# The first layer's input read by columns from memory, and its first query and key blocks walked together

## The chip, the core and the metric

The kernel runs on one core of a Trainium2 chip. TensorE (PE) multiplies, ScalarE (ACT) rounds and evicts, VectorE (DVE) makes remainders, masks and small transposes, GpSimd (POOL) rotates queries and keys and makes some remainders, and SyncE (SP) issues nearly all transfers. The metric is the time of one execution in device microseconds. Before the change the median of three runs is 840.39 us (839.6 to 840.73).

## The reference, cut to what matters

```
hn   = rms_norm(x, pre_norm_g[0])                  # x: 256 rows x 2048 columns, float32
proj = hn @ attn_w_in                              # 2048 x 8192
q, k, v, z = split(proj, 4)                        # 16 heads of 128 columns each
q, k = rope(q), rope(k)
o = causal_softmax(q k^T / sqrt(128)) v
x = x + rms_norm((o * silu(z)) @ attn_w_out, post_norm_g[0])
# then a second layer: gated convolution over 31 rows, layer norm, silu gate, w_out, again added to x
```

The root mean square scales a row, so it can be applied after the product: the kernel multiplies x times the gain by the weights, and scales each row when the sums leave PSUM. What the change touches is the head of this: how x comes in, how it is turned, and when the row scale is known.

## The kernel before, in words

All products are float32 in three passes: each operand is split into a rounded part (hi, written by ACT) and the remainder (lo, written by DVE, or by POOL in some later stages), and PE adds hi*hi, hi*lo and lo*hi. The weights stream through `raw` (four buffers of 1 MB, one SP transfer each), and are split by *slices*: a slice is two tiles of 128 rows of the inner dimension by 512 columns, so a buffer holds two slices. Eight slices make one block of 512 columns; a slice is 12 products of 512 columns. Each slice has one of four slots in `w_hi` and `w_lo`, so ACT can start on slice s only when PE has finished slice s-4. A slice's number below counts from 0 within a group.

The first layer goes through four groups of four heads. In a group, slices 0 to 7 make the queries, 8 to 15 the keys, 16 to 23 the values, 24 to 31 the gate. The order of each engine's work is written out by hand, slice by slice. In a group, ACT scales and evicts the query block (`block_rows`, lines 809 to 815) once it is complete; POOL then turns it by the rope tables (`rotate`, lines 1577 to 1597: four products with the sines, two with the cosines, one sum); DVE transposes the result in four steps of four 32-row transposes, one step behind each of four slices' remainders, beginning at slice `TURN_Q`. The keys follow in the same way with `TURN_K`. DVE runs in order: when a step waits for POOL, the remainder of the next slice waits behind it, and PE waits for that remainder.

In the first group the start is special. x comes in rows, PE turns it (`input_T`, four transposes of 128 by 128 for each pair of tiles), ACT writes `xT_hi` from PSUM with the gain, DVE `xT_lo`. The first two slices are done tile by tile (`FINE = 2`, `tile_products`), the next two by passes (`staged_products`). ACT squares the rows of x in between (eight pieces, two for each quarter of the columns) for the row scale; DVE sums them (`mean_of_parts`), POOL takes the inverse root into `rms[0]`, and the query block is evicted only then. Gains, biases and convolution taps come in by rows and are turned by PE as well.

Of the kernel before, what the change touches and what calls it, by code (L numbers as in the profile page):

```python
# [23 lines left out]
P = 128  # L24
SEQ = 256
D = 2048
# [27 lines left out]
NVEC = 5 * KT  # L54
ROOT_AT = 27
# [5 lines left out]
SPLIT_AFTER = ((), (), (2,), (3,), (4, 5), (6,), (7, 8), (9,))  # L61
FINE = 2
SQUARES_AFTER = (1, 2, 3, 5)
STAGED = 4
# [21 lines left out]
DW_ROWS = TAPS * KT // 4  # L86


def build(nc, x, pre_g, post_g, w_in0, w_out0, w_in1, b_in, w_dw, b_dw, ln_g, ln_b, w_out1, b_out,
# [5 lines left out]
    with ctx:  # L95
# [27 lines left out]
        uT_lo = at("uT_lo", B + 16 * KB, [P, KT, SEQ], f32r)  # L123
        c_row = at("c_row", B, [P, MT, D])
# [30 lines left out]
        vec_rows = at("vec_rows", C, [NVEC, P])  # L155
        dw_rows = at("dw_rows", C + 512, [DW_ROWS, 4, P])
        pre_rows = at("pre_rows", C + 2 * KB + 512, [NPRE, P])
# [38 lines left out]
        tile_in = [sem(f"tile_in{i}") for i in range(2 * FINE - 1)]  # L196
        half_in = sem("half_in")
        x_in = [sem(f"x_in{i}") for i in range(6)]
        tile_xhi, tile_xlo = sem("tile_xhi"), sem("tile_xlo")
        tile_whi, tile_wlo = sem("tile_whi"), sem("tile_wlo")  # L200
        tile_T = sem("tile_T")
        ident_in = sem("ident_in")
        pre_in = sem("pre_in")
        vec_in = sem("vec_in")
        dw_in = sem("dw_in")
# [3 lines left out]
        vec_T = sem("vec_T")  # L209
        vec_ready = sem("vec_ready")  # L210
# [93 lines left out]
        def x_chunk(h):  # L304
            return h if h < 4 else 2 + h // 2

        def of_tile(t, even, pair, count):

            return (even, t // 2 + 1) if t % 2 == 0 else (pair, count)

# [9 lines left out]
        def _(sp):  # L320
# [15 lines left out]
            def x_load(first, last):  # L336
                c = slice(first * SEQ, (last + 1) * SEQ)
                sp.dma_start(xrow[:, :, c], xv[:, :, c]).then_inc(x_in[x_chunk(first)], 16)

            def w_load(n, first, last, done):  # L340

                k = 2 * SL_K * n
                sp.dma_start(raw[:, n, first:last + 1], wv[:, k + first:k + last + 1, 0:NCOL]).then_inc(done, 16)
# [6 lines left out]
            w_load(0, 2, 2, tile_in[2])  # L350
            w_load(0, 3, 3, raw_ready[0])
            x_load(2, 2)
            w_load(1, 0, 1, half_in)
            x_load(3, 3)
            w_load(1, 2, 3, raw_ready[1])
            x_load(4, 5)
            load(S_QKVZ, 0, 32, 2, w_in0[0], 0)
            x_load(6, 7)
            load(S_QKVZ, 0, 32, 3, w_in0[0], 0)
            load(S_QKVZ, 0, 32, 4, w_in0[0], D)  # L360

            for v, rows, src in ((V_BA, 2 * KT, b_in), (V_BDW, KT, b_dw), (V_LNG, KT, ln_g), (V_LNB, KT, ln_b)):
                sp.dma_start(vec_rows[v - NPRE:v - NPRE + rows, :], src.rearrange("l (t c) -> (l t) c", c=P)
                             ).then_inc(vec_in, 16)
# [3 lines left out]
            sp.dma_start(dw_rows[:], w_dw[0].rearrange("k (t c) -> (k t) c", c=P)  # L368
                         .rearrange("(q r) c -> r q c", r=DW_ROWS)).then_inc(dw_in, 16)

            for j in range(5, 16):
                load(S_QKVZ, 0, 32, j, w_in0[0], (j // 4) * D)
# [63 lines left out]
        def _(pe):  # L436
# [54 lines left out]
            def input_T(layer, h):  # L491

                if layer == 0:
                    pe.wait_ge(x_in[x_chunk(h)], 16)
                    if h == 1:
                        pe.wait_ge(vec_ready, 1)
                    if h >= 4:
                        pe.wait_ge(xlo_ready, h - 3)
                else:
                    for m in range(MT):  # L500
                        pe.wait_ge(x1_ready[m], h + 1)
                    pe.wait_ge(xlo_ready, units(h - 4, 1))
                if layer == 0 and h < FINE:
                    for t in (2 * h, 2 * h + 1):
                        for m in range(MT):
                            last = nc.tensor.transpose(X[t][:, m * P:(m + 1) * P], xrow[:, m, t * P:(t + 1) * P],
                                                       ident[:])
                        last.then_inc(xT_done if t % 2 else tile_T, 1)
                else:
                    pair_T(xrow, X[h % 4], 2 * h).then_inc(xT_done, 1)  # L510

            def staged_products(h):

                slot = h % RING
                n = h + 1
                passes = [(xT_hi, w_hi, ((xhi_ready, n), (hi_ready[slot], rounds(S_QKVZ, 0, 0, h)))),
                          (xT_lo, w_hi, ((xlo_ready, n),)),
                          (xT_hi, w_lo, ((lo_ready[slot], rounds(S_QKVZ, 0, 0, h)),))]
                for p, (xs, ws, needs) in enumerate(passes):
                    for which, count in needs:  # L520
                        pe.wait_ge(which, count)
                    for i in range(SL_K):
                        k = SL_K * h + i
                        for m in range(MT):
                            last = nc.tensor.matmul(acc[:, 0, m], xs[:, k, m * P:(m + 1) * P],  # L525
                                                    ws[:, slot, i], start=(k == 0 and p == 0), stop=False)
                last.then_inc(w_used[slot], 1)

            def tile_products(t):
# [3 lines left out]
                passes = [(xT_hi, w_hi, (of_tile(t, tile_xhi, xhi_ready, n), of_tile(t, tile_whi, hi_ready[slot], 1))),  # L533
# [11 lines left out]
            def first_block():  # L545

                tile_products(0)
                input_T(0, 1)
                tile_products(1)
                tile_products(2)  # L550
                input_T(0, 2)
                tile_products(3)
                input_T(0, 3)
                for h in range(FINE, SLICES):
                    if h < STAGED:
                        staged_products(h)
                    else:
                        pe.wait_ge(xlo_ready, h + 1)
                        slice_products(S_QKVZ, 0, 32, h, xT_hi, xT_lo)
                    if h + 2 < SLICES:  # L560
                        input_T(0, h + 2)
# [38 lines left out]
            def group(g, first):  # L600

                for s in range(SLICES if first else 0, 4 * SLICES):
                    if s % SLICES == 0 and not (first and s < 2 * SLICES):
                        pe.wait_ge(rows_out, 4 * g + s // SLICES - 1)
                    slice_products(S_QKVZ, g, 32, s, xT_hi, xT_lo)
                    if s == VALUES_AT and not first:
                        values(g - 1)
                    if s == 9 and first:
# [1056 lines left out]
```

## Time and profile before

| | |
|---|---|
| median of three runs | 840.39 us |
| the profiled execution | 840.96 us |
| its span, first to last instruction | 839.2 us |
| PE busy | 829.8 us, 99% of the span |
| DVE busy | 713.0 us, 85% |
| share of PE in the chain that ended last | 98% |
| mean granted clock | 0.997 |

An engine's rows in the timeline begin with start and duration in us from the span's start; instructions of one kind that follow each other closely are merged into one row with their count. In the chain of waits each row is a piece of the path that set the end. The windows give for a stretch the busy time of each engine, the granted clock, the busy share of the DMA engines and the rate in GB/s. In the listing of transfers the last number is the time from issue to landing.

### The profile page before, as it was taken

Reading aid. Unit: us, or ns where it says so; the run is one execution under the profiler, and the core shown is the slowest. Engines: PE = TensorE matmul, PEld = TensorE weight load, DVE = VectorE, ACT = ScalarE, POOL = GpSimd, SP = SyncE. Lnnn points to the kernel's source line nnn. Section 1 sums busy time; section 2 is a strip of 40 time slices with the busy share of each in tenths; the row PEclk is TensorE's granted clock in tenths of the full one; section 3 lists DMA queues with packets and bytes.
Section 4 is the critical chain, followed back from the end, with each engine's and each line's share of the span. In section 5 each row is a group of like instructions: output and inputs, shape, how many; then the busy total and the mean of one; then the engine's idle time right before and its main releaser. Section 6 shows DMA issues by size and latency. Waiting matters only on the chain.

```text
span 839.2 us, 10950 instructions
## 1 busy us (share of the span) xinstructions
PE 829.8 (99%) x3807; PEld 687.6 (82%) x3807; DVE 713.0 (85%) x1234; ACT 426.3 (51%) x589; POOL 343.1 (41%) x173
## 2 busy tenths in 40 slices
PE   9999999999999999999999999999999999999996
PEld 6888888888888888888888888888888888888885
DVE  5688799988999799979847649999999999898655
ACT  6744535455444734454446574444545454575542
POOL 0343005500441004500000198888888878894001
PEclk9999999999999999999999999999999999999998
DMA  9956656656567555756455485556555646566522
GB/s 316 318 157 202 193 150 177 195 181 196 154 176 224 171 178 153 219 175 243 171 195 197 150 285 192 182 195 200 182 172 198 200 151 201 196 215 246 196 100 100
DMA packets 97945, 161.62 MB, mean 193 GB/s; under 512 B 3348, under 2 KB 38772, under 8 KB 97396
## 3 DMA queue, kind: packets, MB, share of 16 engines
q1 hardware_dynamic: 97572, 160.87, 59.3%
q8 instruction: 20, 0.33, 0.2%
q10 hardware_dynamic: 336, 0.28, 0.1%
q14 instruction: 17, 0.14, 0.0%
HBM read 159.04 MB, written 2.10 MB: 192 GB/s over the span
## 4 chain that ended last, share of the span: by engine, by line
PE 98%; DMA 0%; DVE 0%; ACT 0%; issue 0%; DVEq 0%; POOL 0%; SPq 0%
PE acc L459 29%; PE acc L460 29%; PE acc L461 29%; PE X L469 1%; PE acc L444 1%; PE acc L446 1%; PE acc L445 1%; PE X L459 1%; PE X L460 1%; PE X L461 1%; PE acc L525 1%; PE acc L540 1%; DMA xrow<-in_x 0%; PE acc L779 0%; PE acc L778 0%; PE acc L777 0%
## 5 line engine op out<-in xcount | busy, mean ns | idle before, releaser
L806 ACT ACTIVATE w_hi<-raw 128x1024 fp32r<-128x1024 f32 x282 | 298.6, 1060 | 339.3 <-PE acc L461 326.5
L459 PE MATMUL acc<-w_hi,xT_hi 128*128 128x512 f32 x864 | 339.1, 392 | 0.0
L461 PE MATMUL acc<-w_hi,xT_lo 128*128 128x512 f32 x864 | 336.9, 390 | 0.0
L460 PE MATMUL acc<-w_lo,xT_hi 128*128 128x512 f32 x864 | 336.7, 390 | 0.0
L1112 DVE TENSOR_TENSOR w_lo<-raw,w_hi 128x1024 fp32r<-128x1024 f32 x180 | 242.2, 1362 | 69.6 <-ACT w_hi L806 67.2
L1609 POOL TENSOR_TENSOR w_lo<-raw,w_hi 128x1024 fp32r<-128x1024 f32 x102 | 248.4, 2443 | 45.1 <-ACT w_hi L806 45.0
L461 PEld LDWEIGHTS acc<-w_hi,xT_lo 128*128 128x128 f32 x864 | 162.3, 188 | 33.9
L459 PEld LDWEIGHTS acc<-w_hi,xT_hi 128*128 128x128 f32 x864 | 162.4, 188 | 33.2 <-DVE xT_lo L1131 0.3
L460 PEld LDWEIGHTS acc<-w_lo,xT_hi 128*128 128x128 f32 x864 | 162.4, 188 | 32.7
L1402 DVE SCALAR_TENSOR_TENSOR X<-u_pad,taps,X 128x256 f32<-128x256 f32 x464 | 183.7, 478 | 3.5 <-ACT X L1019 3.5
L1572 POOL TENSOR_TENSOR small<-small 128x1 f32<-128x1 f32 (+1 forms) x7 | 4.3, 618 | 221.5 <-DVE small L1329 122.9
L1586 POOL TENSOR_TENSOR rope_t<-q_row,sin_t 128x256 f32<-128x256 f32 x16 | 15.3, 990 | 178.7 <-ACT q_row L814 178.7
L459 PE MATMUL acc<-w_hi,vT_hi 128*128 128x512 f32 x112 | 43.8, 391 | 0.0
L460 PE MATMUL acc<-w_lo,vT_hi 128*128 128x512 f32 x112 | 43.6, 390 | 0.0
L461 PE MATMUL acc<-w_hi,vT_lo 128*128 128x512 f32 x112 | 43.6, 390 | 0.0
L1214 DVE STREAM_TRANSPOSE pT<-probs 32x384 f32<-32x384 f32 x64 | 36.3, 567 | 1.0
L1586 POOL TENSOR_TENSOR rope_t<-k_row,sin_t 128x256 f32<-128x256 f32 x16 | 16.2, 1045 | 44.3 <-ACT k_row L814 44.3
L459 PE MATMUL acc<-w_hi,uT_hi 128*128 128x512 f32 x80 | 31.2, 391 | 0.0
L461 PE MATMUL acc<-w_hi,uT_lo 128*128 128x512 f32 x80 | 31.2, 390 | 0.0
L460 PE MATMUL acc<-w_lo,uT_hi 128*128 128x512 f32 x80 | 31.2, 390 | 0.0
L1204 DVE STREAM_TRANSPOSE kT<-k_row 32x256 f32<-32x256 f32 x64 | 27.9, 436 | 1.0
L1204 DVE STREAM_TRANSPOSE uT<-u_row 32x256 f32<-32x256 f32 x64 | 27.9, 436 | 1.0
(165 smaller groups left out, 800.4 us busy)
## 6 DMA issues: line engine op xcount, KB each, us to landing
raw<-in_w_in SPq DMA_DIRECT2D x78, 1024.0 KB, 5.3
raw<-in_w_in SPq DMA_DIRECT2D x66, 512.0 KB, 4.5
raw<-in_w_out SPq DMA_DIRECT2D x32, 1024.0 KB, 5.1
gpost<-in_post_g SPq DMA_DIRECT2D x2, 1024.0 KB, 5.7
brow<-in_b_in SPq DMA_DIRECT2D x1, 2048.0 KB, 10.4
out<-xrow SPq DMA_DIRECT2D x6, 256.0 KB, 2.8
xrow<-in_x SPq DMA_DIRECT2D x4, 256.0 KB, 5.9
raw<-in_w_in SPq DMA_DIRECT2D x4, 256.0 KB, 4.5
```

Source lines behind the costliest of these rows:

```text
L444: nc.tensor.matmul(a, hi[:, k, rows], wh[:, i], start=(k == 0), stop=False)
L445: nc.tensor.matmul(a, hi[:, k, rows], wl[:, i], start=False, stop=False)
L459: nc.tensor.matmul(a, hi[:, k, rows], w_hi[:, slot, i], start=(k == 0), stop=False)
L460: nc.tensor.matmul(a, hi[:, k, rows], w_lo[:, slot, i], start=False, stop=False)
L461: last = nc.tensor.matmul(a, lo[:, k, rows], w_hi[:, slot, i], start=False, stop=(k == KT - 1 or n == pause))
L806: nc.scalar.activation(w_hi[:, slot], raw[:, u % LOADS, 2 * half:2 * half + 2], ACT.Copy).then_inc(hi_ready[slot], 1)
L1112: nc.vector.tensor_tensor(lo_of(first, it, s), raw[:, u % LOADS, 2 * half:2 * half + 2], hi_of(first, it, s).bitcast(f32), ALU.subtract).t ...
L1204: last = nc.vector.transpose(dst[b * BLK:(b + 1) * BLK].rearrange("p h (m c) -> p m h c", m=MT) [:, :, :, a * BLK:(a + 1) * BLK], row[a * ...
L1214: last = nc.vector.transpose(pT[b * BLK:(b + 1) * BLK].rearrange("p h (i c) -> p (h i) c", i=3) [:, :, a * BLK:(a + 1) * BLK], probs[a * B ...
L1402: nc.vector.scalar_tensor_tensor(out=cT[:, tile] if last else part, in0=u_pad[:, tile, k:k + SEQ], scalar=taps[:, tile + k * KT:tile + k * ...
L1586: last = nc.gpsimd.tensor_tensor(t[:, :, o], v[:, :, w], sin_t[:, m:m + 1, o].to_broadcast([P, G, HALF]), ALU.mult)
L1609: nc.gpsimd.tensor_tensor(w_lo[:, slot], raw[:, u % LOADS, 2 * half:2 * half + 2], w_hi[:, slot].bitcast(f32), ALU.subtract).then_inc(lo_r ...
```

## The change

x is read twice: once already by columns, `x_col` (128 partitions by 16 tiles by 256 rows, laid out so in memory), which ACT and DVE split directly, and later by rows, for the squares and the residual. PE's transposes of x in the first layer go, and so do those of gains, biases and taps, which come in by columns too. The first loads are spread over two queues: ACT issues the vectors and two pieces of `x_col`, SP the rest. The four quarters of x by rows come behind the sixth weight buffer and between the next two, and the squares behind slices 10, 11 and 12. In the first group the queries and keys are walked in turn over the first eight tiles of x, pair by pair, then the rest of the queries, then the rest of the keys; so the query block is complete after slice 11 and not 7. It is evicted behind slice 14's rounding (11 before), and turned from slice 17 on (15 before).

```
-FINE = 2
-SQUARES_AFTER = (1, 2, 3, 5)
-STAGED = 4
+X_CHUNKS = ((0, 1), (1, 2), (2, 4), (4, 8), (8, 12), (12, KT))
+ROW_SQUARES_AT = {10: (0,), 11: (1,), 12: (2, 3)}
+FIRST_MEAN_AT = 13
+FIRST_EVICT_Q, FIRST_TURN_Q = 14, 17
+FINE = 1
+FIRST_ORDER = tuple([(b, i) for i in range(SLICES // 2) for b in (0, 1)]
+                    + [(b, i) for b in (0, 1) for i in range(SLICES // 2, SLICES)])
+FIRST_Q_LAST = 11
...
@@ SP @@
-            sp.dma_start(ident[:], identity).then_inc(ident_in, 16)
-            x_load(0, 0)
+            col_load(0)
             w_load(0, 0, 0, tile_in[0])
             w_load(0, 1, 1, tile_in[1])
-            x_load(1, 1)
...
+            w_load(1, 0, 1, raw_ready[0])
+            w_load(2, 0, 1, half_in[0])
+            w_load(3, 0, 1, raw_ready[1])
+            col_load(3)
+            w_load(4, 0, 1, half_in[1])
+            w_load(5, 0, 1, raw_ready[2])
+            w_load(6, 0, 1, half_in[2])
+            w_load(7, 0, 1, raw_ready[3])
+            col_load(4)
+            load(S_QKVZ, 0, 32, 4, w_in0[0], 0, 2)
+            col_load(5)
+            load(S_QKVZ, 0, 32, 5, w_in0[0], 0, 3)
+            row_load(0)
+            row_load(1)
+            load(S_QKVZ, 0, 32, 6, w_in0[0], D, 2)
+            row_load(2)
             sp.dma_start(cos_t[:], rope_cos).then_inc(rope_in, 16)
             sp.dma_start(sin_t[:], rope_sin).then_inc(rope_in, 16)
             sp.dma_start(mask[:], causal).then_inc(rope_in, 16)
-            sp.dma_start(dw_rows[:], w_dw[0].rearrange("k (t c) -> (k t) c", c=P)
...
+            load(S_QKVZ, 0, 32, 7, w_in0[0], D, 3)
+            row_load(3)
+            for j in range(8, 16):
                 load(S_QKVZ, 0, 32, j, w_in0[0], (j // 4) * D)
+                if j == 8:
+                    sp.dma_start(ident[:], identity).then_inc(ident_in, 16)
+                    sp.dma_start(taps[:], tap_cols).then_inc(taps_in, 16)
@@ PE @@
-                tile_products(0)
-                input_T(0, 1)
...
+                for t in range(2 * FINE):
+                    tile_products(t)
+                for s in range(FINE, SLICES):
+                    staged_products(s)
...
-            keep_clock(4)
-            pe.wait_ge(ident_in, 16)
-            pe.wait_ge(pre_in, 16)
-            nc.tensor.transpose(X[3][:, 0:NPRE], pre_rows[:], ident[0:NPRE, 0:NPRE]).then_inc(vec_T, 1)
-            keep_clock(3)
-            input_T(0, 0)
-            keep_clock(2)
+            keep_clock(8)
@@ ACT @@
+            act.dma_start(vec[:], vectors).then_inc(vec_in, 16)
+            for i in (1, 2):
+                a, b = X_CHUNKS[i]
+                act.dma_start(x_col[:, a:b], x_cols[:, a:b]).then_inc(col_in[i], 16)
...
+            def column_high(h):
+                act.wait_ge(col_in[col_chunk(2 * h)], 16)
+                for t in (2 * h, 2 * h + 1):
+                    last = nc.scalar.activation(xT_hi[:, t], x_col[:, t], ACT.Copy,
+                                                scale=vec[:, V_PRE0 + t:V_PRE0 + t + 1])
+                last.then_inc(xhi_ready, 1)
...
+            def first_squares(n):
+                act.wait_ge(row_in[n], 16)
+                for m in range(MT):
+                    squares(junk0[:], xrow[:, m, n * NCOL:(n + 1) * NCOL], m, n, MT * n + m)
...
-                    if s == 11:
+                    if first:
+                        for n in ROW_SQUARES_AT.get(s, ()):
+                            first_squares(n)
+                    if s == (FIRST_EVICT_Q if first else EVICT_Q):
@@ DVE @@
-            dve.wait_ge(rope_in, 48)
-            mean_of_parts(8, 1)
...
+                    if s == FIRST_MEAN_AT and first:
+                        mean_of_parts(8, 1)
+                        dve.wait_ge(rope_in, 48)
...
+                    turn_q = FIRST_TURN_Q if first else TURN_Q
+                    if s in range(turn_q, turn_q + 4):
```

On PE the program begins as follows before the change (`idle` are products on zeros that only keep the engine running; `pre_rows` are the gains).

```order
L567 MATMUL acc<-idle 128x512 [waits const_set]
L567 MATMUL acc<-idle 128x512 x3
L574 MATMUL X<-ident,pre_rows 128x32 [waits pre_in,ident_in]
L567 MATMUL acc<-idle 128x512 x3
L506 MATMUL X<-ident,xrow 128x128 [waits x_in0]
L506 MATMUL X<-ident,xrow 128x128 x3
L567 MATMUL acc<-idle 128x512 x2
L540 MATMUL acc<-w_hi,xT_hi 128x512 [waits tile_whi,tile_xhi]
```

And after it:

```order
L563 MATMUL acc<-idle 128x512 [waits const_set]
L563 MATMUL acc<-idle 128x512 x7
L547 MATMUL acc<-w_hi,xT_hi 128x512 [waits tile_whi,tile_xhi0]
L547 MATMUL acc<-w_hi,xT_hi 128x512
L547 MATMUL acc<-w_hi,xT_lo 128x512 [waits tile_xlo]
```

The transposes are gone, one idle product fewer runs, and the first real product waits for the rounded weight tile and the rounded columns alone.

On ACT the stretch around the eviction of the first group's queries is this before the change (`junk` takes the squares, of which only the sum is kept).

```order
L806 ACTIVATE w_hi<-raw 128x1024 [waits w_used1,raw_ready0]
L843 ACTIVATE junk_71,small<-xrow 128x512 [waits ssq_ready,x_in4] x2
L843 ACTIVATE junk_71,small<-xrow 128x512 [waits ssq_ready,x_in5] x2
L806 ACTIVATE w_hi<-raw 128x1024 [waits w_used2,raw_ready1]
L806 ACTIVATE w_hi<-raw 128x1024 [waits w_used3,raw_ready1]
L814 ACTIVATE q_row<-acc,small 128x512 [waits w_used3,rms_ready]
```

After it, from the rounding of slice 12 to that of slice 15:

```order
L790 ACTIVATE w_hi<-raw 128x1024 [waits w_used0,raw_ready2]
L835 ACTIVATE junk_72,small<-xrow 128x512 [waits ssq_ready,row_in2]
L835 ACTIVATE junk_72,small<-xrow 128x512 [waits ssq_ready]
L835 ACTIVATE junk_72,small<-xrow 128x512 [waits ssq_ready,row_in3]
L835 ACTIVATE junk_72,small<-xrow 128x512 [waits ssq_ready]
L790 ACTIVATE w_hi<-raw 128x1024 [waits w_used1,raw_ready2]
L790 ACTIVATE w_hi<-raw 128x1024 [waits w_used2,raw_ready3]
L798 ACTIVATE q_row<-acc,small 128x512 [waits w_used3,rms_ready]
L798 ACTIVATE q_row<-acc,small 128x512
L790 ACTIVATE w_hi<-raw 128x1024 [waits w_used3,raw_ready3]
```

The last squares now stand directly ahead of the rounding of slice 13 and wait for the last quarter of x by rows (`row_in3`), and three slices later than before the queries are evicted.

On DVE the first group's turning of the queries stands behind the remainder of slice 15 before the change.

```order
L1112 TENSOR_TENSOR w_lo<-raw,w_hi 128x1024 [waits hi_ready3]
L1204 STREAM_TRANSPOSE qT<-q_row 32x2x4x32 [waits rope_step]
L1204 STREAM_TRANSPOSE qT<-q_row 32x2x4x32 x3
L1112 TENSOR_TENSOR w_lo<-raw,w_hi 128x1024 [waits hi_ready0]
L1204 STREAM_TRANSPOSE qT<-q_row 32x2x4x32 x4
L1112 TENSOR_TENSOR w_lo<-raw,w_hi 128x1024 [waits hi_ready1]
```

After it, it stands behind the remainder of slice 17:

```order
L1092 TENSOR_TENSOR w_lo<-raw,w_hi 128x1024 [waits hi_ready1]
L1193 STREAM_TRANSPOSE qT<-q_row 32x2x4x32 [waits rope_step]
L1193 STREAM_TRANSPOSE qT<-q_row 32x2x4x32 x3
L1092 TENSOR_TENSOR w_lo<-raw,w_hi 128x1024 [waits hi_ready2]
L1193 STREAM_TRANSPOSE qT<-q_row 32x2x4x32 x4
L1092 TENSOR_TENSOR w_lo<-raw,w_hi 128x1024 [waits hi_ready3]
```

The first transpose of the four steps waits for POOL's third step on the queries (`rope_step`); the remainder of slice 18 (`hi_ready2`) stands behind it.

## Rows read from the trace of the kernel before

**Rows 1.** The page: busy us (share of the span) and instructions, by engine.
```profile
PE 829.8 (99%) x3807; PEld 687.6 (82%) x3807; DVE 713.0 (85%) x1234; ACT 426.3 (51%) x589; POOL 343.1 (41%) x173
```

**Rows 2.** The chain of waits, first 30 us: start us, us, what.
```profile
1.18 3.92 DMA xrow<-in_x
...
9.37 0.44 PE X L506 x4
...
24.57 0.44 PE X L469 x4
```

**Rows 3.** Timeline of PE: start us, us, engine line op, tiles, shapes, count.
```profile
1.00 1.89 PE L567 MATMUL acc<-idle 128*128 128x512 bf16 x4 [1.00 <-POOL small L1567]
...
6.62 1.35 PE L540 MATMUL acc<-w_hi,xT_hi 128*128 128x512 f32 x2
...
39.05 0.59 PE L613 MATMUL X<-ident,dw_rows 124*128 124x124 f32 x4
```

**Rows 4.** Timeline of ACT.
```profile
5.85 0.63 ACT L872 ACTIVATE w_hi<-raw 128x512 fp32r<-128x512 f32 x1 [2.37 <-DMA raw<-in_w_in]
...
30.74 0.63 ACT L843 ACTIVATE junk<-xrow 128x512 f32<-128x512 f32 x1
...
31.55 0.63 ACT L843 ACTIVATE junk<-xrow 128x512 f32<-128x512 f32 x1
...
34.90 1.24 ACT L814 ACTIVATE q_row<-acc,small 128x512 f32<-128x512 f32 x2
...
45.21 1.06 ACT L806 ACTIVATE w_hi<-raw 128x1024 fp32r<-128x1024 f32 x1 [1.66 <-PE acc L461]
...
56.09 1.06 ACT L806 ACTIVATE w_hi<-raw 128x1024 fp32r<-128x1024 f32 x1 [1.66 <-PE acc L461]
```

**Rows 5.** Issue of one weight buffer, the eighth, in the timeline of SP.
```profile
28.16 0.37 SPq L330 DMA_DIRECT2D raw<-in_w_in  x1
```

**Rows 6.** Transfers issued from 28.1 to 28.2 us: KB, us to landing.
```profile
raw<-in_w_in SPq DMA_DIRECT2D x1, 1024.0 KB, 8.3
```

**Rows 7.** Transfers issued from 1.6 to 1.7 us: KB, us to landing.
```profile
raw<-in_w_in SPq DMA_DIRECT2D x1, 256.0 KB, 4.1
```

**Rows 8.** Windows: stretch, length, PE, PEld, DVE, ACT, POOL busy, clock, DMA share, GB/s.
```profile
5.00:10.00 5.00, 4.85 (x18) 3.83 (x19) 2.56 (x5) 1.89 (x5) 0.00 (x0) 1.00 1.01 316
...
20.00:25.00 5.00, 4.98 (x26) 4.00 (x26) 4.30 (x6) 3.65 (x7) 0.00 (x0) 1.00 0.93 316
25.00:30.00 5.00, 5.00 (x26) 4.09 (x25) 4.25 (x7) 4.48 (x8) 0.00 (x0) 1.00 0.97 296
30.00:35.00 5.00, 5.00 (x24) 4.14 (x23) 2.49 (x5) 4.72 (x12) 0.71 (x1) 1.00 1.05 388
```

**Rows 9.** Timeline of DVE: the mean, then turning steps and remainders.
```profile
33.19 0.16 DVE L1144 TENSOR_REDUCE small<-small 128x2 f32<-128x8 f32 x1 [1.90 <-ACT junk L843]
...
48.09 1.77 DVE L1204 STREAM_TRANSPOSE qT<-q_row 32x256 f32<-32x256 f32 x4
49.90 1.23 DVE L1112 TENSOR_TENSOR w_lo<-raw,w_hi 128x1024 fp32r<-128x1024 f32 x1
...
68.06 3.22 DVE L1112 TENSOR_TENSOR w_lo<-raw,w_hi 128x1024 fp32r<-128x1024 f32 x1 [1.49 <-ACT w_hi L806]
...
154.48 9.02 DVE L1112 TENSOR_TENSOR w_lo<-raw,w_hi 128x1024 fp32r<-128x1024 f32 x4
```

**Rows 10.** Timeline of POOL: the root, the queries' rotation, the keys' last step.
```profile
33.71 0.71 POOL L1572 TENSOR_TENSOR small<-small 128x2 f32<-128x2 f32 x1 [32.73 <-DVE small L1139]
...
36.22 3.90 POOL L1586 TENSOR_TENSOR rope_t<-q_row,sin_t 128x256 f32<-128x256 f32 x4 [1.79 <-ACT q_row L814]
...
43.82 3.26 POOL L1595 TENSOR_TENSOR q_row<-q_row,rope_t 128x1024 f32<-128x1024 f32 x1
...
67.80 2.40 POOL L1595 TENSOR_TENSOR k_row<-k_row,rope_t 128x1024 f32<-128x1024 f32 x1
```

More of the change, by code:

```diff
@@ L302, in units, with col_chunk, units_T, of_tile_x @@
             return SLICES + (RING * m + h + 1 if h < RING else RING + h + 1)
-        def x_chunk(h):
-            return h if h < 4 else 2 + h // 2
+        def col_chunk(t):
+            return next(i for i, (_, end) in enumerate(X_CHUNKS) if t < end)
+        def units_T(h, m):
+            return units(h, m) - SLICES
         def of_tile(t, even, pair, count):
             return (even, t // 2 + 1) if t % 2 == 0 else (pair, count)
+        def of_tile_x(t, count):
+            return (tile_xhi[t // 2], 1) if t % 2 == 0 else (xhi_ready, count)
         def loaded(first, it, per, s):
@@ L334, in _, with w_load @@
             wv = cols(w_in0[0])
[L336 to L343, printed above, removed]
-            sp.dma_start(ident[:], identity).then_inc(ident_in, 16)
-            x_load(0, 0)
+            def w_load(place, first, last, done):
+                b, part = FIRST_ORDER[place]
+                k, c = SL_K * part, SL_K * (place % 2)
+                sp.dma_start(raw[:, place // 2, c + first:c + last + 1],
+                             wv[:, k + first:k + last + 1, b * D:b * D + NCOL]).then_inc(done, 16)
@@ L489, in acc_free, with input_T, staged_products @@
                     pe.wait_ge(y_ready, MT * (o - 31))
[L491 to L516, printed above, removed]
+            def input_T(h):
+                for m in range(MT):
+                    pe.wait_ge(x1_ready[m], h + 1)
+                pe.wait_ge(xlo_ready, units(h - 4, 1))
+                pair_T(xrow, X[h % 4], 2 * h).then_inc(xT_done, 1)
+            def staged_products(s):
+                slot = s % RING
+                b, part = FIRST_ORDER[s]
+                n = part + 1
+                passes = [(xT_hi, w_hi, ((xhi_ready, n), (hi_ready[slot], rounds(S_QKVZ, 0, 0, s)))),
                           (xT_lo, w_hi, ((xlo_ready, n),)),
-                          (xT_hi, w_lo, ((lo_ready[slot], rounds(S_QKVZ, 0, 0, h)),))]
+                          (xT_hi, w_lo, ((lo_ready[slot], rounds(S_QKVZ, 0, 0, s)),))]
                 for p, (xs, ws, needs) in enumerate(passes):
@@ L807, in high, with block_rows @@
                                      ).then_inc(hi_ready[slot], 1)
-            def block_rows(first, it, per, s, dst, scale, func=ACT.Copy):
-                act.wait_ge(w_used[RING - 1], rounds(first, it, per, s))
+            def block_rows(first, it, per, s, dst, scale, func=ACT.Copy, last_slice=None):
+                act.wait_ge(w_used[RING - 1], rounds(first, it, per, last_slice or s))
                 par = ((first + s) // SLICES) % 2
@@ L1125, in row_low, with input_low @@
                 last.then_inc(xlo_ready, 1)
-            def input_low(layer, n, vcol):
-                dve.wait_ge(xhi_ready, units(n, 1) if layer else n + 1)
+            def input_low(n):
+                dve.wait_ge(xhi_ready, units(n, 1))
                 for c in range(2):
@@ L1283, in out0_rows @@
                     dve.wait_ge(gpost0_in, 16)
+                    for n_in in range(NG):
+                        dve.wait_ge(row_in[n_in], 16)
                 for m in ms:
```

197 lines of the change are left out of this document (78 added, 119 removed).

## The prediction

> **What bounds the kernel now.** I read the page's busy shares first: PE is busy 99% of the span, and no other engine is near that [rows 1]. So an edit gains only where it takes work or a wait from PE, and loses wherever it makes PE wait. From there I went to the chain of waits over the first 30 us, because the change touches nothing else. The reader is to see there that the chain enters through the first piece of x, which lands at 1.18 + 3.92 = 5.1 us, and then stays on PE, with a piece of 0.44 for each group of four transposes of x [rows 2]. Then the timeline of ACT gives PE's pitch without PE's rows: the roundings of slices 15 and 19 start at 45.21 and 56.09, each released by the slice four before, so four slices take 10.88, one 2.72, and slice 15 ends at about 56.0 [rows 4]. Sixteen slices at 2.72 are 43.5; PE stands 12.5 behind a start at zero.
>
> **What goes from PE.** The sum is made against the profiled execution, 840.96 (span 839.2 and 1.76 around it; the median of the runs is 0.57 lower).
> - Eight groups of transposes go. The first lies ahead of the first product, and counts below; seven at 0.44 [rows 2] are 3.1.
> - The transposes of taps and vectors go from behind slice 9: 0.6 [rows 3].
> - The start. Before, the first product begins at 6.62 [rows 3], 0.14 after the rounding that starts at 5.85 and takes 0.63 [rows 4]. That rounding waited for the weight tile, third in the queue (issued 1.66, 4.1 to landing [rows 7]: 5.75). Now the tile is second in its queue, behind 128 KB. It lands between 5.1 (what the second transfer took before [rows 2]) and 5.75; I take 5.4, near the middle, and the first product at 6.2: 0.4 gained, with 0 and 0.7 as ends. The vectors and the first columns are smaller than what landed by 5.1, and are hidden.
> - The clock. The idle products run at the lower level (four in 1.89 us, 1.2 and not 2.4 GHz; the first real products too, two in 1.35) [rows 3]. Eight of them without a break now end near 4.5, and then PE is empty for 1.7 us, where before it was interrupted thrice for less. If the full clock comes at once, up to six products save 0.2 each, 1.2; if it comes one slice later, 12 lose 0.2 each, 2.4. I take 0.
>
> So until the middle of the first group PE should run 4.1 earlier: slice s begins at 8.4 + 2.72 s. That it does so needs the weights in time. Walking queries and keys in turn asks for 512 KB of weights and on average 128 KB of columns per 2.72 us at first, 241 GB/s, against 388 that the engines moved [rows 8]: hidden.
>
> **What is late next.** x now comes twice, so 2 MB more are in the same queues, and the rows, from which the squares come, are the last. Up to the last quarter of the rows the queues hold 8,192 KB of weights, 2,048 by columns, 2,048 by rows and 376 of vectors and tables, 12,664 in all. Before, up to the eighth weight buffer they held 10,928 KB, and that landed at 28.16 + 8.3 = 36.5 [rows 5, 6]. The extra 1,736 KB (1.78 MB) at 388 GB/s [rows 8] take 4.6: 41.1. Less: from 5 to 10 us, with pieces of 1 KB, the rate was 316 and not 388, 0.36 MB or 0.9 us [rows 8]; from 20 to 30 us the transfers of vectors and taps in short pieces held it to 316 and 296, 0.82 MB or 2.1 us, of which about half goes, since tables and mask stay. That gives 39.2. The bounds: 41.1 if nothing of this is saved; and 36.4, if from 5.0 us (0.8 MB moved) all goes at 388: (12.97 - 0.8) MB in 31.4 us. I take 38.7, between them and near the sum.
>
> From there the chain is:
> - the last two squares, each 0.81 (31.55 less 30.74) [rows 4]: 40.3;
> - rounding of slice 13, 1.06 [rows 4]: 41.4; its remainder, 1.23 and 0.1 for the hand-over [rows 9]: 42.7. PE wants it at 8.4 + 35.4 = 43.8, so no wait yet;
> - mean and root, 33.19 to 34.42 [rows 9, 10], 1.2: 43.9; eviction of the queries, 1.24 [rows 4]: 45.3 with hand-over. PE ended slice 11 at 41.0, so it is the row scale that holds the eviction back, by 4;
> - the rotation, 36.22 to 47.08 [rows 10], 10.9: 56.2.
>
> Three roundings of 1.06 after the eviction, slice 17 is rounded at 48.5, so DVE has its remainder done by about 51 and stands at the first turning step until 56.2. This is the wait that counts. Queued behind it on DVE is the remainder of slice 18: turning 1.77, then 1.23 if alone [rows 9], 59.2. PE wants it at 57.4. Then three more rounds of turning and remainder are due every 2.72: alone each takes 1.77 + 1.23 + hand-overs, 3.05, so 0.3 more than PE gives.
>
> But they are not alone. The keys' rotation starts as the queries' ends, and there the remainders stretch: one at 68.06 took 3.22 and ended 1.08 after POOL's sum (67.80 + 2.40) did, and four in a row beside POOL took 9.02, 2.26 each [rows 9, 10]. The turning steps do not stretch, 1.77 beside POOL's work or not. At 2.26 a round is 4.1, 1.4 more than PE gives. So slice 18 begins between 59.2 and 60.3, I take 59.9, 2.5 late; the three rounds cost 0.9 (all alone) to 4.2 (all beside POOL), I take 2.4 since the rotation covers about two of them. Together 4.9, against 4.1 gained: 0.8 slower, 841.8 for a profiled execution, **841.2** for the median of runs.
>
> Note what this makes of the first list. Once slice 18 waits, it begins when the rows let it, whenever PE began. The start and the clock, with their bounds, then only lengthen or shorten the wait. The term that counts is the landing of the last rows, one for one.
>
> *A rule against the row.* The four in 9.02 give a mean price for a remainder beside POOL [rows 9]. The Trainium skill, SBUF — State Buffer, section "SBUF: two separate sides", has a sharper rule: a VectorE instruction with two inputs in SBUF and a GpSimd one lock each other out for the whole instruction. The trace agrees with it at 68.06, where the remainder ends one remainder after POOL's sum. By the rule the round that meets the keys' sum would cost about 2.4 alone, the others 0.3 to 0.5, 3.2 in all and not 2.4: 842.0.
>
> **Other edits, at nothing.** Walking order, `FINE = 1`: no product is added. ACT's part of x now reads SBUF in place of PSUM, two instructions of the same size per pair. The squares move but keep their number. `ident` and `taps` come some 25 us later and are first used in the second half of the kernel. The second layer's transposes stay.
>
> **Rivals.**
> - *Faster: the rows come early and the remainders slip in between POOL's steps.* With the rows at 36.4 the rotation ends at 53.9 and slice 18 has its remainder at 56.9, before PE wants it (57.4); the rounds then cost 0.9 less 0.5 of lead. Then 3.7 of the 4.1 stay: 836.7; with the start and clock at their good ends up to 1.9 more. For it: 388 GB/s held for long stretches [rows 8]. Against it: tables, mask and the first columns still come in short pieces, and the stretches that had such pieces ran at 296 and 316 [rows 8]. 0.28.
> - *Slower: the rows come late.* At 40.5 the rotation ends at 58.0, slice 18 begins at 61.7, 4.3 late, and with 2.9 to 3.2 for the rounds that is 7.3 less 4.1, 3.2 slower: 843.6. It decides from a landing of about 39.6 on, with the rounds as taken above, or from 38.8 with the price of the rule. For it: the 41.1 of the plain sum. 0.30.
> - *The change doesn't do what it says*: the start is no earlier and the clock stays at the low level through the first slice. PE would begin the middle of the group up to 2.8 later than above; as long as slice 18 waits by 2.5 that costs almost nothing, so it lies within the forecast, and caps the faster rival at 838.
>
> **How the numbers follow.** A difference under 0.2% (1.7 us) cannot be told from none. Forecast, about level with a small loss: 0.42, its own range 839.2 to 842.1. Faster 0.28, 835.8 to 838.7. Slower 0.30, 842.1 to 845. The range reaches into both and leaves out about one in ten on either side: 836.0 to 844.0.
>
> **What would show it.** Right: no transposes of x ahead of the first layer's products; the last row load of x landing at 38 to 39.5; ACT's eviction of the queries 3 us or more after PE finished slice 11; DVE idle about 5 us before the first turning step; PE idle, or with long gaps, at slices 18 to 21 (57 to 72 us), released by DVE's `w_lo`; remainders of over 2 us there. Wrong: a rotation that begins at 43 or earlier, or remainders at 1.23 beside the turning, with PE unbroken to 90 us: then the gain of 4 us stays and the forecast falls.

## The result, and the profile after

The median of eight runs is 842.55 us (842.15 to 844.7), beside 840.15 us for the kernel before (839.53 to 840.73) on the same chip: a ratio of 1.0031, 95% interval 1.0021 to 1.0040. The change makes the kernel slower by 0.3%, 2.4 us. The profiled execution took 842.53, its span 840.7; before, 840.96 and 839.2.

The page of the kernel after, busy time by engine, and further down the shares of the chain that ended last:

```profile
PE 826.5 (98%) x3768; PEld 682.7 (81%) x3768; DVE 710.5 (85%) x1233; ACT 426.3 (51%) x586; POOL 341.6 (41%) x173
...
PE 94%; DVE 2%; POOL 1%; DMA 1%; issue 1%; ACT 0%; SPq 0%; DVEq 0%; POOLq 0%; ACTq 0%
```

PE has 3.3 us less work than before [rows 1], and the span is 1.5 longer. The chain, 98% PE before, now spends 6% elsewhere: somewhere PE is held. The start is not the place. The chain of waits in its first 30 us:

```profile
2.12 5.98 DMA raw<-in_w_in
8.13 1.07 ACT w_hi L790
9.33 19.31 PE acc L532 x84
28.64 0.23 PE acc L479
```

Slices 1 to 7 run in one piece of 19.31 us, and slice 8 begins at 28.64. That is 6.9 behind a slice pitch of 2.72 from zero, where before it was 12.5 once the taps behind slice 9 were done. PE has gained 5.6, in this execution. Timeline of PE, the idle products, the first two products, and slice 18:

```profile
1.00 3.59 PE L563 MATMUL acc<-idle 128*128 128x512 bf16 x8 [1.00 <-POOL small L1563]
5.41 0.70 PE L547 MATMUL acc<-w_hi,xT_hi 128*128 128x512 f32 x2 [0.82 <-ACT w_hi L853]
...
59.85 0.80 PE L479 MATMUL acc<-w_hi,xT_hi 128*128 128x512 f32 x1 [3.08 <-DVE w_lo L1092]
```

The first product is at 5.41 and not 6.62, and two of them take 0.70 and not 1.35 [rows 3]. The rounded tile that it waits for, on ACT:

```profile
4.64 0.63 ACT L853 ACTIVATE w_hi<-raw 128x512 fp32r<-128x512 f32 x1 [0.99 <-DMA raw<-in_w_in]
```

Then at 59.85 stands what took it back: 3.08 us without work, for the remainder of slice 18. Followed back, the wait comes from the rows of x. SP's issue of their last quarter, and the listing of that transfer (KB, us to landing):

```profile
25.74 3.46 SPq L361 DMA_DIRECT2D xrow<-in_x  x1
```
```profile
xrow<-in_x SPq DMA_DIRECT2D x1, 512.0 KB, 12.9
```

25.74 and 12.9 make 38.6. Timeline of ACT, the square that waits for it and the eviction of the queries:

```profile
38.63 0.63 ACT L835 ACTIVATE junk<-xrow 128x512 f32<-128x512 f32 x1 [3.55 <-DMA xrow<-in_x]
...
44.34 1.27 ACT L798 ACTIVATE q_row<-acc,small 128x512 f32<-128x512 f32 x2 [2.33 <-POOL small L1568]
```

Timeline of POOL, the root, the start and end of the queries' rotation, and the keys' sum:

```profile
42.74 1.56 POOL L1568 TENSOR_TENSOR small<-small 128x2 f32<-128x2 f32 x1 [41.76 <-DVE small L1129]
45.69 4.80 POOL L1582 TENSOR_TENSOR rope_t<-q_row,sin_t 128x256 f32<-128x256 f32 x4 [1.38 <-ACT q_row L798]
...
54.05 2.41 POOL L1591 TENSOR_TENSOR q_row<-q_row,rope_t 128x1024 f32<-128x1024 f32 x1
...
64.09 2.40 POOL L1591 TENSOR_TENSOR k_row<-k_row,rope_t 128x1024 f32<-128x1024 f32 x1
```

The rotation ends at 56.46; before, the sum ran at 43.82 and nobody waited for it [rows 10]. Timeline of DVE:

```profile
56.49 1.78 DVE L1193 STREAM_TRANSPOSE qT<-q_row 32x256 f32<-32x256 f32 x4 [4.93 <-POOL q_row L1591]
58.30 1.49 DVE L1092 TENSOR_TENSOR w_lo<-raw,w_hi 128x1024 fp32r<-128x1024 f32 x1
...
61.63 1.23 DVE L1092 TENSOR_TENSOR w_lo<-raw,w_hi 128x1024 fp32r<-128x1024 f32 x1
...
64.70 2.87 DVE L1092 TENSOR_TENSOR w_lo<-raw,w_hi 128x1024 fp32r<-128x1024 f32 x1
...
69.43 4.63 DVE L1092 TENSOR_TENSOR w_lo<-raw,w_hi 128x1024 fp32r<-128x1024 f32 x4
```

DVE stood 4.93 us at the first turning step, and the remainder of slice 18, queued behind it, ran from 58.30. The remainder of slice 20 at 64.70 took 2.87 and ended one remainder after POOL's sum (66.49), as at 68.06 before [rows 9]. From 58.30 three rounds of remainder and turning lead to the remainder of slice 21 at 69.43: 11.13 us, where PE gives 8.16. The third round, which meets POOL's sum, takes 4.73 of them, the other two 3.33 and 3.07. Last, the windows around the stop (stretch, length, PE busy, granted clock, DMA share, GB/s):

```profile
57.00:59.80 2.80, 0.00 (x0) 0.98 0.00 0
59.80:61.00 1.20, 1.15 (x3) 0.50 0.00 0
...
62.00:63.00 1.00, 1.00 (x3) 0.50 0.00 0
63.00:64.00 1.00, 1.00 (x6) 0.95 0.03 4
```

The granted clock falls to 0.50, 1.2 of 2.4 GHz, after 3.08 us in which PE did nothing, and slice 18 takes 4.4 us (59.85 to 64.2) and not 2.72. Whether that costs anything is a question for an experiment: DVE is late with slice 20 anyhow.

### The profile page after: what moved, and what is told of

It is laid out like the page before. It is cut to its first block, busy times and chain, and to the rows that moved or that the text cites. A ratio compares the mean times of both kernels' runs of the same rounds, so it can differ in the third digit from the quotient of the medians.

```text
span 840.7 us, 10874 instructions
## 1 busy us (share of the span) xinstructions
PE 826.5 (98%) x3768; PEld 682.7 (81%) x3768; DVE 710.5 (85%) x1233; ACT 426.3 (51%) x586; POOL 341.6 (41%) x173
## 4 chain that ended last, share of the span: by engine, by line
PE 94%; DVE 2%; POOL 1%; DMA 1%; issue 1%; ACT 0%; SPq 0%; DVEq 0%; POOLq 0%; ACTq 0%
PE acc L479 27%; PE acc L481 27%; PE acc L480 27%; PE acc L532 2%; DVE w_lo L1092 1%; PE acc L464 1%; PE acc L466 1%; PE acc L465 1%; PE X L481 1%; PE X L479 1%; PE X L480 1%; DVE qT L1193 1%; PE X L489 1%; DMA raw<-in_w_in 1%; POOL rope_t L1582 1%
## 5 line engine op out<-in xcount | busy, mean ns | idle before, releaser
L479 PE MATMUL acc<-w_hi,xT_hi 128*128 128x512 f32 x848 | 333.4, 393 | 4.1 <-DVE w_lo L1092 4.0
L481 PE MATMUL acc<-w_hi,xT_lo 128*128 128x512 f32 x848 | 330.7, 390 | 0.0
L480 PE MATMUL acc<-w_lo,xT_hi 128*128 128x512 f32 x848 | 330.6, 390 | 0.0
L479 PEld LDWEIGHTS acc<-w_hi,xT_hi 128*128 128x128 f32 x848 | 159.6, 188 | 38.7 <-DVE w_lo L1092 4.9
L481 PEld LDWEIGHTS acc<-w_hi,xT_lo 128*128 128x128 f32 x848 | 159.5, 188 | 33.5
L480 PEld LDWEIGHTS acc<-w_lo,xT_hi 128*128 128x128 f32 x848 | 159.7, 188 | 32.4
L1193 DVE STREAM_TRANSPOSE qT<-q_row 32x256 f32<-32x256 f32 x64 | 27.9, 436 | 6.0 <-POOL q_row L1591 4.9
```

What stands on the lines that cost most here:

```text
L479: nc.tensor.matmul(a, hi[:, k, rows], w_hi[:, slot, i], start=(k == 0), stop=False)
L480: nc.tensor.matmul(a, hi[:, k, rows], w_lo[:, slot, i], start=False, stop=False)
L481: last = nc.tensor.matmul(a, lo[:, k, rows], w_hi[:, slot, i], start=False, stop=(k == KT - 1 or n == pause))
L1193: last = nc.vector.transpose(dst[b * BLK:(b + 1) * BLK].rearrange("p h (m c) -> p m h c", m=MT) [:, :, :, a * BLK:(a + 1) * BLK], row[a * ...
```

## The experiments

Theory A throughout: the loss is the queue of DVE in the first group, last rows, row scale, rotation, turning, remainders; the start's gain is kept wherever that queue does not stop PE. Rivals: the change has made PE's products or the transfers slower in general (B), or the fallen clock is what costs (C). Ratios are to the kernel before, run on the same chip. Differences between two variants are differences of their medians; some of these come from different chips, on which the kernel before had medians of 839.9 to 840.17.

### The turning three slices later (turn20)

```
-FIRST_EVICT_Q, FIRST_TURN_Q = 14, 17
+FIRST_EVICT_Q, FIRST_TURN_Q = 14, 20
```

> One number: the first group's queries are turned from slice 20 on, not 17. Theory A (the loss is DVE's order: the remainder of slice 18 queued behind a turning step that waits for the rotation): the rotation still ends near 56.4, but DVE has three more slices of remainders done ahead of the step, so PE runs unbroken from slice 8 to 23 and keeps the 5.6 us that it was ahead at slice 8; turning of queries and keys then stands without a break on DVE, eight rounds, and the keys' last step ends near 81.7 where PE reaches the scores at 80.3, so up to 1.4 is given back there: 835.5 to 837.5. Theory B (the loss comes from reading x twice, transfers that make PE's operands late): no change, 842.5.

Measured: 839.86 us (839.33 to 843.71), ratio 1.0004 (0.9992 to 1.0015). Faster than the changed kernel by 2.7, though by less than A said. PE's waits of the first 95 us in its trace (us in total, times, longest), then two rows of DVE:

```profile
PE X L573 <- DVE kT L1193: 1.9, 1, 1.9
```
```profile
46.52 12.79 DVE L1092 TENSOR_TENSOR w_lo<-raw,w_hi 128x1024 fp32r<-128x1024 f32 x6 [2.85 <-ACT w_hi L790]
...
82.38 1.79 DVE L1193 STREAM_TRANSPOSE kT<-k_row 32x256 f32<-32x256 f32 x4
```

There is no wait for a remainder any more. But six remainders in a row beside POOL's rotation took 12.79, 2.13 each, so the turning began at 59.23 and not at 56.4, and the keys, turned last, ended at 84.17; the first scores waited 1.9 for them. The wait moved and shrank. Part of what A missed lies at the start: in this execution slice 1 began at 10.45 and not at 9.33, so 4.5 of the 5.6 were there to be kept. A holds, my sizes for it did not.

### The last rows earlier and later (rows_early, rows_late)

```
 row_load(2)
+row_load(3)                # rows_early: here
 ... cos_t, sin_t, mask, eighth weight buffer ...
-row_load(3)
 ... ninth weight buffer ...
+row_load(3)                # rows_late: here instead
```

> The last quarter of x by rows is issued ahead of the tables and the eighth weight buffer, 1.3 MB earlier in the queue; nothing else. Theory A: it lands 3.2 us earlier (35.4 and not 38.6), and eviction, rotation, turning and slices 18 to 21 follow one for one until PE's own pace holds: 839.3 (838.5 to 840.2). Theory B (which bytes come first does not matter, the bytes are the same): 842.5. Theory C (the clock's fall behind the 3.1 us stop at slice 18 is the price): the stop becomes about 0.5, the clock stays high and 1.6 more is gained: below 838.

> The changed kernel with the last quarter of x's rows issued one place later, behind the ninth 1 MB weight buffer: the dose in the other direction to rows_early. 1 MB at 388 GB/s is 2.7 us of transfer. Theory A: the landing of the last rows sets the middle of the first group one for one: they land at 41 to 42, TensorE's wait at slice 18 grows from 3.1 to 5.8, and the time is 845.2 (844.5 to 846). Rival B: what limits slice 18 is POOL's or VectorE's sum of work, the rows alone are hidden: 842.5 to 843.5.

Measured: early 839.43 us (838.53 to 840.26), ratio 0.9993 (0.9983 to 1.0003); late 845.03 (844.86 to 845.33), ratio 1.0055 (1.0040 to 1.0070). Timeline of ACT in rows_late, then PE's waits there:

```profile
41.21 0.63 ACT L835 ACTIVATE junk<-xrow 128x512 f32<-128x512 f32 x1 [6.27 <-DMA xrow<-in_x]
```
```profile
PE acc L479 <- DVE w_lo L1092: 4.8, 3, 2.4
```

In rows_late the rows land 2.6 later, and the time is 2.5 longer: one for one. The place differs from what A said. PE already waits 2.4 at slice 13, whose rounding stands behind the squares, and only 1.9 at slice 18; the end is the same, since slice 18 begins when the rotation allows. In rows_early, whose square of the last quarter ran at 35.44 without a wait, ACT, DVE and PE:

```profile
40.50 1.27 ACT L798 ACTIVATE q_row<-acc,small 128x512 f32<-128x512 f32 x2 [0.55 <-PE acc L481]
```
```profile
52.76 1.78 DVE L1193 STREAM_TRANSPOSE qT<-q_row 32x256 f32<-32x256 f32 x4 [3.66 <-POOL q_row L1591]
54.57 1.61 DVE L1092 TENSOR_TENSOR w_lo<-raw,w_hi 128x1024 fp32r<-128x1024 f32 x1
...
61.77 2.86 DVE L1092 TENSOR_TENSOR w_lo<-raw,w_hi 128x1024 fp32r<-128x1024 f32 x1
...
66.49 4.63 DVE L1092 TENSOR_TENSOR w_lo<-raw,w_hi 128x1024 fp32r<-128x1024 f32 x4
```
```profile
59.98 0.50 PE L479 MATMUL acc<-w_hi,xT_hi 128*128 128x512 f32 x1 [0.55 <-DVE w_lo L1092]
...
64.69 0.50 PE L479 MATMUL acc<-w_hi,xT_hi 128*128 128x512 f32 x1 [1.69 <-DVE w_lo L1092]
```

The time is in the range of A. Now PE's slice 11, not the rows, releases the eviction: in this execution rows still earlier would not help. DVE still stands 3.66 at the first turning step, but the remainder of slice 18 (54.57) is done before PE comes for it. PE waits at slices 19 and 20 instead: the three rounds from 54.57 to 66.49 take 11.92, and the remainder at 61.77 still stretches to 2.86. The granted clock stayed at 1.00 here, and the time is not below 838 as C said.

### PE kept at work before slice 18 (keep18)

```
+if first and s == 18:
+    for _ in range(10):      # products of zero into a free bank
+        nc.tensor.matmul(X[0][:], idle[:], ...)
```

> Ten products on zeros into an unused bank ahead of slice 18, in the time in which PE stands there, so that the clock does not fall. Theory A: slice 18 takes 2.7 and not 4.4 us, but slices 20 and 21 still wait for their remainders, which DVE ends at 67.6 and 70.7, so the time does not move: 842.5 plus or minus 0.4. Theory C (the clock's fall is a price of its own): 1.6 less, 840.9.

Measured: 842.63 us (842.25 to 843.19), ratio 1.0030 (1.0018 to 1.0041): no gain. Windows of keep18 over slice 18, then PE's waits:

```profile
59.80:64.00 4.20, 4.20 (x21) 1.00 0.00 0
```
```profile
PE acc L479 <- DVE w_lo L1096: 1.3, 1, 1.3
```

The clock stays at 1.00, and PE then waits 1.3 at slice 20 where it had waited 0.51. C falls: the low clock filled time in which DVE was late anyhow. In this execution slice 1 had begun at 11.73, 2.4 later than in the changed kernel's, and still PE had 1.3 to spare at slice 20 and the span is the same 840.7: here the start does not reach the end either.

### POOL's sum in two pieces (split_sum, split_keep)

```
-last = nc.gpsimd.tensor_tensor(row[:], row[:], rope_t[:], ALU.add)
+for m in range(MT):
+    last = nc.gpsimd.tensor_tensor(row[:, m], row[:, m], rope_t[:, m], ALU.add)
```

> POOL's last step of each rotation, one sum of 128 by 1024, as two of 128 by 512. Theory A with the exclusive port: the remainder of slice 20, which waits for the whole sum of the keys (2.87 us), waits for one half at most, 1.7 to 1.9: 1.0 less, and 0.1 to 0.2 more on the queries' rotation: 841.6 (841.2 to 842.0). Theory D (the remainder is slow beside POOL whatever POOL does, a matter of shared bandwidth): the remainder still takes over 2.5, 842.6.

> The changed kernel with POOL's sums in two pieces (split_sum) and the ten products of zero ahead of slice 18 (keep18, which also leave TensorE's clock at the higher level). In split_sum alone the sum's pieces shortened the remainder of slice 20 from 2.87 to 1.74, but the kernel gained only 0.5, and the granted clock was at its lower level until about 65.3. Theory A: there the lower clock bounded what the remainders no longer did; with the clock kept high the whole 1.1 shows: 841.4 (841.1 to 841.7). Rival B: the next turning steps bound it, clock or not: 842.0 as split_sum.

Measured: split_sum 842.02 us (841.43 to 842.74), ratio 1.0023 (1.0013 to 1.0033); with the zero products as well, 841.45 (840.82 to 841.93), ratio 1.0012 (1.0003 to 1.0021). The remainder of slice 20 in split_sum, POOL's sum of the keys beside it, and the windows there:

```profile
64.48 1.74 DVE L1092 TENSOR_TENSOR w_lo<-raw,w_hi 128x1024 fp32r<-128x1024 f32 x1
```
```profile
63.86 3.51 POOL L1592 TENSOR_TENSOR k_row<-k_row,rope_t 128x512 f32<-128x512 f32 x2
```
```profile
59.60:65.30 5.70, 5.68 (x14) 0.50 0.23 42
```

The remainder shrinks from 2.87 to 1.74, because it now waits for half a sum: what stretched it was one whole instruction of POOL. That is the exclusive lock of the Trainium skill, SBUF — State Buffer, section "SBUF: two separate sides", and the trace agrees with it (2.87 against 1.74 with the instruction cut in two). POOL pays in turn: its two halves took 3.51 together, and the whole sum 2.40. So D falls. But the kernel gained only 0.5, and in the profiled run the clock stayed at 0.50 for 5.7 us. In split_keep:

```profile
59.80:64.00 4.20, 3.56 (x14) 1.00 0.00 0
```

With the clock high the median is 1.1 below the changed kernel, as A said, though the intervals of the two ratios still touch (at 1.0021). Against split_sum alone the gain is 0.6, and there the intervals overlap. So keep18 shows that the clock costs nothing while DVE is the later one; that it costs something as soon as DVE is not is likely, but not shown clear of the noise.

### Two waits removed together (best19, best_nosplit)

best19 has rows_early, the split sums and `FIRST_TURN_Q = 19`; best_nosplit is the same without the split.

> The changed kernel with three edits put together: the last quarter of x's rows issued before the tables and the eighth weight buffer (rows_early), the queries' first turning step behind slice 19 and not 17, and POOL's sums in two pieces of 128x512 (split_sum). Theory A: these three waits are what took back the 5.6 us that TensorE gained by 28.6 us. With the rows landed by 35.4 the rotation ends near 52.8 as in rows_early; with two remainders more ahead of the first turning step, slices 18 and 19 are not held up by it, and the remainder beside the keys' sum costs 1.7 and not 2.9. What is left is at most one wait of 0.5 at slice 20 or 21: offset of TensorE 6.9 to 7.4 after slice 21 instead of 13.95, so 835.5 to 836.5. Rival B: the stretch is limited by VectorE's sum of work (remainders and turning steps, 3.05 a round or more beside POOL, against 2.72 of TensorE), and moving the turning later only moves the wait: 838.5 to 839.5, as rows_early. Rival C: the keys' turning, now later, makes the scores wait, as in turn20: 837.5.

> best19 without the split sums: the last rows early and the first turning step of the queries behind slice 19, with POOL's sum again one piece of 128x1024. It tells what the split is worth once the other two waits are gone. In best19's trace the remainder of slice 20 ran from 64.01 to 65.78 beside the keys' sum, and TensorE took slice 20 at 65.8 without a gap, so there was hardly any lead left. Theory A: with the sum whole that remainder again ends 1.1 later, and TensorE waits for it: 836.9 (836.4 to 837.5). Rival B: the stretch has slack by now, the lock falls on nothing: 835.8, as best19. It also parts the gain of the turning moved by two slices from that of the split, since rows_early alone came to 839.4: by A the move is worth 2.5, by B all 3.6.

Measured: best19 835.77 us (835.35 to 837.53), ratio 0.9948 (0.9934 to 0.9961); best_nosplit 836.4 (836.02 to 836.59), ratio 0.9951 (0.9937 to 0.9964). Both beat the kernel before by 0.5% and the changed kernel by more. PE's waits of best_nosplit in the first 95 us, its windows over the stretch that had the stops, and the remainder beside the keys' sum:

```profile
PE acc L563 <- POOL small L1563: 1.0, 1, 1.0
PE acc L547 <- ACT w_hi L853: 1.0, 1, 1.0
```
```profile
57.00:72.00 15.00, 15.00 (x68) 1.00 0.53 159
```
```profile
63.06 2.86 DVE L1092 TENSOR_TENSOR w_lo<-raw,w_hi 128x1024 fp32r<-128x1024 f32 x1
```

PE has no wait left after its first product. The remainder is still stretched to 2.86, and nobody waits for it: with the turning two slices later it is that of slice 22, not 20 as I wrote in the expectation, and it ends about 1.9 before PE wants it (67.84). So in this trace the split has nothing to gain, as rival B says. The times alone don't decide it: 836.4 is where A's range begins, and the ratios of the two kernels (0.9948 and 0.9951) overlap. The move by two slices is worth 3.0 over rows_early.

### The walk and the second queue, from best19 (best_nowalk, best_oneq)

```
-FIRST_ORDER = tuple([(b, i) for i in range(SLICES // 2) for b in (0, 1)] + ...)
-FIRST_Q_LAST = 11
+FIRST_ORDER = tuple([(b, i) for b in (0, 1) for i in range(SLICES)])   # best_nowalk
+FIRST_Q_LAST = 7
...
-act.dma_start(vec[:], vectors)      # best_oneq: this and the two column loads
+sp.dma_start(vec[:], vectors)       # of ACT's queue go to SP, in turn with the weights
```

> The same as best19, but the first group walks all slices of the queries first and then all of the keys, each slice after its own pair of columns of x; the column and weight loads stand in the order in which that needs them. It tells what the walking of queries and keys in turn is worth. Theory A: without the walk each slice of 2.72 us asks for 256 KB of columns and 256 KB of weights, and TensorE waits for columns at slices 1 to 3 (estimate: the transfers bring 316 GB/s in this stretch, 1.7 us per slice's data, after the first at 4.6, so the waits are short): 0.3 to 1.5 us at the start; but the queries end four slices earlier (slice 7 and not 11), so their rotation is bound by the rows of x alone: 836.3 to 837.5. Rival B: the early transfers keep up, and the walk is worth nothing: 835.5 to 836.3. Rival C: splitting of x falls behind on ACT and VectorE, three or more us: over 838.5.

> The same as best19, but with the first loads all on SP's queue (vectors, then the columns of x and the weights in turn), none on ACT's. It tells what the second queue is worth. Theory A: SP issues one load after another, some 0.5 us each before and after, so with two more loads ahead the first weight tile comes 0.5 to 1.3 later: 836.3 to 837.5. Rival B: the transfers, not the issues, bound the start; the first weight tile lands as early, and the time is that of best19 to 0.2.

Measured: without the walk 837.84 us (837.55 to 838.55), ratio 0.9973 (0.9962 to 0.9984); with one queue 836.89 (836.0 to 837.56), ratio 0.9956 (0.9941 to 0.9971). best_nowalk on PE and on ACT:

```profile
14.55 1.17 PE L531 MATMUL acc<-w_hi,xT_hi 128*128 128x512 f32 x4 [1.78 <-ACT w_hi L789]
```
```profile
12.55 0.91 ACT L826 ACTIVATE xT_hi<-x_col,vec 128x256 fp32r<-128x256 f32 x2 [2.91 <-DMA x_col<-in_x_cols]
```

At slice 2 PE waits 1.78, at bottom for columns of x. By the medians the walk, with the order of loads that goes with it, is worth 2.1, somewhat more than my 0.3 to 1.5. The profiled executions don't show all of it: they are 837.93 and, the slowest of best19, 837.53. That the walk would gain nothing in the changed kernel, where slice 18 waits, follows from the above but was not run. The second queue I leave open: with one queue the first product is no later (5.45, below); the rounding of the third weight transfer starts at 10.33, where best19 had 10.20 and best_nosplit 9.17, and the intervals overlap. PE, then ACT:

```profile
5.45 0.70 PE L550 MATMUL acc<-w_hi,xT_hi 128*128 128x512 f32 x2 [1.04 <-ACT w_hi L852]
```
```profile
10.33 1.06 ACT L793 ACTIVATE w_hi<-raw 128x1024 fp32r<-128x1024 f32 x1 [2.80 <-DMA raw<-in_w_in]
```

## Why the prediction was right and where it was wrong

The time, 842.55, lies in the range, 1.35 above the 841.2 forecast and 0.45 above the upper end that I had set for "about level", so among the "slower". The mechanism was the forecast's; sizes were off.

- *What goes from PE: 4.1 forecast, 5.6 measured in the profiled execution.* The first product came at 5.41 and not 6.2: the weight tile was there by 4.64, before the lower bound of 5.1 that I took from another transfer of before. And the clock, priced at 0, was high from the first product; up to 1.2 had been my good end. But this execution is the best of nine. The eight variants that begin with the same instructions as the changed kernel (all but best_nowalk and best_oneq) began slice 1 at 9.74 to 11.73, where the changed kernel had 9.33: gains of 3.2 to 5.2, around the forecast. best19's slice 1:

```profile
11.40 1.17 PE L532 MATMUL acc<-w_hi,xT_hi 128*128 128x512 f32 x4 [0.59 <-ACT w_hi L790]
```

  None of it reached the end as long as slice 18 waited.
- *Landing of the last rows: 38.7 forecast, 38.6 measured.* The bytes in the queues ahead of them, by the rates of before, were enough for the size; that it came to 0.1 is luck, since the sum itself gave 39.2 and 38.7 was a choice between bounds.
- *Rotation's end: 56.2 forecast, 56.46 measured.* Within it the root took 1.56 (0.71 before), and the remainders of slices 15 to 17, beside POOL, 4.97.
- *Slice 18: 59.9 forecast, 59.85 measured.* Also that start and clock "only lengthen or shorten the wait" held: PE, 1.5 ahead of the forecast at slice 8, lost some of that in stops of 0.23 at slice 13, where I had forecast none, and 0.20 at slice 15; it was ready for slice 18 at 56.77 and not 57.4, and waited 3.08 in place of 2.5, with the same start. rows_late confirms that the landing counts one for one.
- *"The three rounds cost 2.4": the step that failed.* They cost 3.0 (11.13 on DVE against 8.16). I had averaged the four remainders beside POOL [rows 9]; the price that I set beside it, 3.2, was the better one. Beyond PE's 2.72 the round that met POOL's sum cost 2.0, the others 0.6 and 0.35. split_sum shows why: the remainder that meets POOL's sum waits for the whole instruction.
- *The median: 0.57 below the profiled execution forecast, none measured.* The profiled execution comes to 842.53, 0.7 above the 841.8 of my sum; the other 0.6 is this correction. The profiled execution of before lay high among its own runs; that of the changed kernel lay on its median. That the stop at slice 18 absorbs what varies at the start, as the equal spans of keep18 and the changed kernel suggest, is a likely reason, not a shown one.
- *The clock.* I considered it at the start only. It fell at slice 18, which I had not forecast, and keep18 shows that it cost nothing there.
- *Rivals.* The faster one rested on rows at 36.4. rows_early had them by 35.44 and came to 839.4, not 836.7. Its step at slice 18 was right: the remainder was done by 56.18, and PE did not wait for it. What it had wrong is the same step as above: it priced the rounds at 0.9, and they took 11.92 on DVE, 3.8 more than PE's 8.16. Only the later turning gives its 836. The slower one priced rows at 40.5 with 843.6; from the measured time and rows_late's one for one I estimate 844.4.

## What to carry to other kernels

A saving at the start of an engine reaches the end only if nothing later in the same stage is held by something else; here the row scale came with the last transfer, and up to 5.6 us turned into a wait. When a transfer is moved back, follow it to the first in-order queue in which a waiting step stands ahead of work for the bottleneck, and move that step behind the work: two edits, one load earlier and one step two slices later, turned a loss of 2.4 into a gain of 3.8. Before a low clock or a stretched instruction is blamed, look at who waits for it. And a start that is read from one execution is one draw: here the same instructions began slice 1 anywhere from 9.33 to 11.73.

## What the runs showed of the hardware

- PE's pace at the start is not the same from run to run. In best_nosplit, after the same eight idle products as in the changed kernel and 0.99 us without work, the first products ran at the pace of the lower level, two in 1.19 and not in 0.70. The granted clock of the windows reads 1.00 there all the same, so the level is read from the durations. Of the nine executions with this start, four began so (turn20, rows_early, keep18, best_nosplit).

```profile
5.58 1.19 PE L547 MATMUL acc<-w_hi,xT_hi 128*128 128x512 f32 x2 [0.99 <-ACT w_hi L853]
```

  It had no wait for the second tile, whereas the profiled run of best19, at the higher level, waited for it:

```profile
PE acc L547 <- ACT w_hi L853: 3.0, 2, 1.9
```

  That span is 835.6, that of best_nosplit 834.8. The second tile's rounding began at 7.86 in best_nosplit and at 8.41 in best19, so there the slow products mostly filled the time until the weights came. Not so in keep18: its slice 1 was rounded by 10.77, and PE, at the slow pace, began it at 11.73.
- The clock's fall at slice 18 lasted 3.2 us in the changed kernel and 5.7 in split_sum, after stops of 3.08 and 3.21. In rows_late it also fell, after stops of 2.42 (slice 13) and 1.91 (slice 18). It did not fall after the stop of 1.95 in turn20 and that of 1.69 in rows_early. Windows of rows_late:

```profile
46.20:49.20 3.00, 3.00 (x9) 0.50 0.93 278
62.50:66.00 3.50, 3.50 (x9) 0.56 0.00 0
```

- VectorE's transposes of 32x256 never stretched beside POOL (1.77 to 1.80 for four in the stretches above). Its remainders, with two inputs, often did (1.49 to 2.87 in the changed kernel), but not every time: the one at 61.63, while POOL was in the keys' cosine products, took 1.23.
